# A decoder trunk on one core, its beginning rearranged: memory rows turned unscaled, first weight unit in pieces, small constants later, bias products moved

## The reference

```python
def rmsnorm(x, g):
    y = xf * lax.rsqrt(jnp.mean(xf * xf, axis=-1, keepdims=True) + EPS)
    return (y * g.astype(jnp.float32)).astype(x.dtype)

def rel_bias(table, dist_tok, heads):          # table (32, 12)
    b = table[t5_bucket(dist_tok)][..., heads]
    return jnp.moveaxis(b, -1, 0).astype(jnp.float32)

mem_n = rmsnorm(mem, mem_norm)                 # 256 memory tokens of 1024
for i in range(2):
    hn = rmsnorm(h, norm_mix[i])               # 256 tokens of 1024
    kv = jnp.einsum('bmd,de->bme', mem_n, w_mem_kv[i])     # 1024 x 512
    p  = jnp.einsum('bsd,de->bse', hn, w_in[i])            # layer 0: 1024 x 1408
    # attention with rel_bias, w_out, then the feed-forward part
```

## Time and profile before

| | us |
|---|---|
| median of three runs | 1511.24 |
| profiled execution, time | 1513.64 |
| profiled execution, span of the trace | 1511.8 |
| PE busy | 1475.3 (98%) |
| DVE busy | 1157.4 (77%) |
| ACT busy | 965.2 (64%) |

### The profile page before, as it was taken

The page is one execution under the profiler, slowest core; times in us unless marked ns, Lnnn a source line. Parts: engine busy times, 40 slices in busy tenths (PEclk is TensorE's granted clock), DMA queues, the critical chain, the costliest instruction groups (busy, mean ns, idle before and its releaser), DMA issues.

```text
span 1511.8 us, 19808 instructions
## 1 busy us (share of the span) xinstructions
PE 1475.3 (98%) x7012; PEld 1219.1 (81%) x7012; DVE 1157.4 (77%) x952; ACT 965.2 (64%) x854; POOL 11.0 (1%) x21
## 2 busy tenths in 40 slices
PE   7999999999999999999999999999999999999997
PEld 6888888887778888788888878888878888887885
DVE  4575544454547788988888888888889888888886
ACT  4554444344544677777777777777777777776775
POOL 0100000000000000000000000000000000000000
PEclk9999999999999999999999999999999999999999
DMA  9633555555540499999989999999999998999993
GB/s 350 234 114 126 195 195 179 188 187 171 190 140 17 165 342 365 354 357 373 357 321 363 372 336 364 376 330 355 365 365 338 377 365 314 367 372 334 372 362 125
DMA packets 184096, 433.70 MB, mean 287 GB/s; under 512 B 6963, under 2 KB 8011, under 8 KB 184060
## 3 DMA queue, kind: packets, MB, share of 16 engines
q1 hardware_dynamic: 182048, 426.80, 78.9%
q0 software_dynamic: 1776, 5.84, 1.2%
q10 hardware_dynamic: 236, 0.57, 0.1%
HBM read 432.10 MB, written 1.09 MB: 287 GB/s over the span
## 4 chain that ended last, share of the span: by engine, by line
PE 90%; DVE 5%; ACT 3%; issue 1%; DMA 1%; DVEq 0%; SPq 0%; ACTq 0%
PE ps L1173 27%; PE ps L1175 27%; PE ps L1174 27%; DVE wlo L703 2%; PE ps L1341 2%; ACT whi L428 2%; PE ps L1294 1%; PE ps L1490 1%; PE ps L1267 1%; DMA raw<-in_swa_w_mem_kv 1%; PE ps L1180 1%; PE ps L1280 1%; PE ps L1514 0%; PE ps L1240 0%; PE ps L1519 0%
## 5 line engine op out<-in xcount | busy, mean ns | idle before, releaser
L703 DVE TENSOR_TENSOR wlo<-raw,whi 128x2048 fp32r<-128x2048 f32 x404 | 918.5, 2290 | 241.2 <-ACT whi L428 241.1
L428 ACT ACTIVATE whi<-raw 128x2048 fp32r<-128x2048 f32 x404 | 772.2, 1914 | 251.4 <-PE ps L1175 249.9
L1173 PE MATMUL ps<-whi,xhi 128*128 128x512 f32 x1328 | 519.2, 391 | 6.2 <-DVE wlo L703 5.2
L1175 PE MATMUL ps<-whi,xlo 128*128 128x512 f32 x1328 | 516.0, 389 | 0.0
L1174 PE MATMUL ps<-wlo,xhi 128*128 128x512 f32 x1328 | 515.9, 388 | 0.0
L1173 PEld LDWEIGHTS ps<-whi,xhi 128*128 128x128 f32 x1328 | 249.3, 188 | 62.5 <-DVE wlo L703 10.3
L1175 PEld LDWEIGHTS ps<-whi,xlo 128*128 128x128 f32 x1328 | 249.3, 188 | 51.7
L1174 PEld LDWEIGHTS ps<-wlo,xhi 128*128 128x128 f32 x1328 | 249.4, 188 | 50.2
L1173 PE MATMUL ps<-whi,thi 128*128 128x512 f32 x560 | 224.3, 400 | 7.9 <-DVE tlo L883 7.9
L1175 PE MATMUL ps<-whi,tlo 128*128 128x512 f32 x560 | 218.9, 391 | 0.0
L1174 PE MATMUL ps<-wlo,thi 128*128 128x512 f32 x560 | 218.3, 390 | 0.0
(11 more groups left out here) (175 smaller groups left out, 636.6 us busy)
## 6 DMA issues: line engine op xcount, KB each, us to landing
raw<-in_moe_up SPq DMA_DIRECT2D x112, 1024.0 KB, 6.9
raw<-in_moe_gate SPq DMA_DIRECT2D x112, 1024.0 KB, 6.8
raw<-in_moe_down SPq DMA_DIRECT2D x112, 1024.0 KB, 6.7
raw<-in_ffn_up SPq DMA_DIRECT2D x14, 1024.0 KB, 5.1
raw<-in_ffn_gate SPq DMA_DIRECT2D x14, 1024.0 KB, 5.1
raw<-in_ffn_down SPq DMA_DIRECT2D x14, 1024.0 KB, 4.9
raw<-in_dil_w_in SPq DMA_DIRECT2D x10, 1024.0 KB, 5.1
raw<-in_swa_w_in SPq DMA_DIRECT2D x4, 1024.0 KB, 15.8
```

What stands on the lines that cost most here:

```text
L428: act.activation(whi[:, c % CUT, 0:span(c)], raw[:, c % RAW, 0:span(c)], ACT.Copy).then_inc(hi_ready, 1)
L703: dve.tensor_tensor(wlo[:, c % CUT, 0:n], raw[:, c % RAW, 0:n], whi[:, c % CUT, 0:n].bitcast(F32), ALU.subtract).then_inc(lo_ready, 1)
L1173: pe.matmul(dst, ahi, bhi, start=start, stop=False)
L1175: return pe.matmul(dst, alo, bhi, start=False, stop=stop)
```

## The change

It does the following:

- PE's first products no longer wait for a constant: they multiply a piece of `hn` that DVE has just set to zero, 7 of them.
- The memory rows are transposed as they come from DRAM. The gain is applied after the transposition, when `xhi` and `xlo` are written: there each row block has one gain number per partition. `xhi` and `xlo` are therefore written in 16 instructions of 128 x 128 each (`mem_hi`, `mem_lo`) and not in 4 of 128 x 512. The gain vector comes as 8 rows of 128 numbers and is turned by one small PE transpose; its copy spread over 128 partitions (512 KB) is no longer loaded.
- Unit 0 is loaded in two halves and cut in four quarters, so that its products can start on the first quarter. Chunk 0 runs unit by unit over both tiles and not tile by tile.
- Only the identity and the reversed identity (256 of the 720 columns of `mats`) are loaded first, from ACT. The other constants, the zero-one matrix and the table are issued by POOL, once unit 1 has landed. `eps` is set by DVE.
- The four bias products become two, one for each layer, with their sums over 33 and 99 rows. They stand between chunk 1 and chunk 2, in banks 4 and 5, and chunk 2 waits until ACT has copied them out (`rows_sb`). The copies stand on ACT ahead of `chunk_out(1)`.
- Units 1 and 2 are both cut by `cut_upto(3)`, ahead of the four `norm_root` calls on ACT and ahead of `gained` on DVE.

The core of the diff (the rest are table shapes, semaphores and index changes that follow from it):

```diff
-            load_chunks(0, 1)
+            mk0 = chunk_w["mk0"]
+            sp.dma_start(raw[:, 0, 0:1024].rearrange("p (k f) -> p k f", k=2), mk0[:, 0:2, 0:512]).then_inc(first_in, 16)
+            sp.dma_start(raw[:, 0, 1024:2048].rearrange("p (k f) -> p k f", k=2), mk0[:, 2:4, 0:512])\
+                .then_inc(raw_full[0], 16)
+            load(1, 0, mk0[:, 4:8, 0:512])
             sp.dma_start(h[:, :, :], x[0].rearrange("(t p) d -> p t d", p=P)).then_inc(x_in, 16)
...
-            load_gain(0)
+            pool.wait_ge(raw_full[1], 16)
+            pool.dma_start(onehot[0][:, :], bias_onehot[0:33, 0, 0:RLEN]).then_inc(onehot_in, 16)
+            pool.dma_start(onehot[1][:, :], bias_onehot[:, 1, 0:RLEN]).then_inc(onehot_in, 16)
+            pool.wait_ge(table_one, 2)
+            pool.dma_start(table[0][0:32, :], rel_bias_table).then_inc(table_in, 16)
+            for g in range(3):
+                pool.dma_start(table[1][32 * g:32 * g + 32, 4 * g:4 * g + 4], rel_bias_table[:, 4 * g:4 * g + 4])\
+                    .then_inc(table_in, 16)
+            pool.dma_start(table[1][96:99, :], bias_onehot[96:99, 1, RLEN:]).then_inc(table_in, 16)
+            pool.dma_start(mats[:, 2 * P:], index_mats[:, 2 * P:]).then_inc(const_in, 16)
             pool.dma_start(sm[:, 496:508], bass.AP(swa_sinks.tensor, swa_sinks.offset, [[0, P], [1, NH]]))\
                 .then_inc(sink_in, 16)
-            pool.wait_ge(rows_sb, 4)
-            pool.dma_start(bias_rows[0], rows[0:NH, 0, :]).then_inc(rows_out, 16)
-            for g in range(3):
-                pool.dma_start(bias_rows[1][4 * g:4 * g + 4, :], rows[0:4, 1 + g, :]).then_inc(rows_out, 16)
-            pool.wait_ge(rows_out, 64)
+            pool.wait_ge(rows_sb, 2)
+            for layer in range(2):
+                pool.dma_start(bias_rows[layer], rows[:, layer, :]).then_inc(rows_out, 16)
...
-            act.dma_start(mats[:, :], index_mats).then_inc(const_in, 16)
+            act.dma_start(mats[:, 0:2 * P], index_mats[:, 0:2 * P]).then_inc(ident_in, 16)
+            act.dma_start(gain_rows[:, :], gains[0].rearrange("(k p) -> k p", k=KT)).then_inc(mem_gain_in, 16)
...
+            def mem_hi(half):
+
+                for t in range(TILES):
+                    b = 2 * t + half
+                    act.wait_ge(tr_done, TR0[T_MEM] + b + 1)
+                    for j in range(4):
+                        kt = 4 * half + j
+                        last = act.activation(xhi[:, kt, t * P:(t + 1) * P], ps[:, b, j * P:(j + 1) * P], ACT.Copy,
+                                              scale=mem_gain[:, kt:kt + 1])
+                    last.then_inc(xhi_ready, 1)
...
-            act.wait_ge(const_in, 16)
+            act.wait_ge(ident_in, 16)
             preload(ACT.Sqrt)
-            act.dma_start(onehot[:, :, :], bias_onehot).then_inc(onehot_in, 16)
-            act.dma_start(table[0:32, :], rel_bias_table).then_inc(table_in, 16)
-            for t in range(TILES):
-                xT_hi(T_MEM, t)
-                cut_upto(t + 1)
+            act.wait_ge(mem_gain_turned, 1)
+            act.activation(mem_gain, ps[:, 4, 0:KT], ACT.Copy).then_inc(mem_gain_ready, 1)
+            act.wait_ge(mem_gain_ready, 1)
+            mem_hi(0)
+            for j in range(4):
+                if j < 2:
+                    act.wait_ge(first_in, 16)
+                else:
+                    act.wait_ge(raw_full[0], 16)
+                act.activation(whi[:, 0, j * 512:(j + 1) * 512], raw[:, 0, j * 512:(j + 1) * 512], ACT.Copy)\
+                    .then_inc(first_hi if j < 3 else hi_ready, 1)
+            nxt[0] = 1
+            mem_hi(1)
+            cut_upto(3)
+            act.wait_ge(eps_set, 1)
             for t in range(TILES):
                 act.wait_ge(mem_in[t], 16)
                 norm_root(0, t, memx)
...
             act.wait_ge(chunk_done, 2)
             xT_hi(T_MIX0, 0)
+            for layer in range(2):
+                act.wait_ge(rows_mm, layer + 1)
+                act.activation(rows[:, layer, :], ps[0:NH, 4 + layer, 0:RLEN], ACT.Copy, scale=8.0).then_inc(rows_sb, 1)
             chunk_out(1, memkv[:, 1, 0, :])
             xT_hi(T_MIX0, 1)
             chunk_out(C_SI, proj[:, 0, 0:CHUNKS[C_SI][1]])
-            act.wait_ge(rows_mm, 1)
-            for g in range(4):
-                n = NH if g == 0 else 4
-                act.activation(rows[0:n, g, :], ps[0:n, g, 0:RLEN], ACT.Copy, scale=8.0).then_inc(rows_sb, 1)
             preload(ACT.Exp)
             for c in range(C_SI + 1, C_SO):
                 chunk_out(c, proj[:, 0, CHUNKS[c][3]:CHUNKS[c][3] + CHUNKS[c][1]])
-            act.wait_ge(rows_out, 64)
+            act.wait_ge(rows_out, 32)
             attention(0)
             for t in range(TILES):
...
+            def mem_lo(half):
+
+                dve.wait_ge(mem_gain_ready, 1)
+                for t in range(TILES):
+                    b = 2 * t + half
+                    dve.wait_ge(xhi_ready, TILES * half + t + 1)
+                    for j in range(4):
+                        kt = 4 * half + j
+                        cols = slice(t * P, (t + 1) * P)
+                        last = dve.scalar_tensor_tensor(xlo[:, kt, cols], ps[:, b, j * P:(j + 1) * P],
+                                                        mem_gain[:, kt:kt + 1], xhi[:, kt, cols].bitcast(F32),
+                                                        ALU.mult, ALU.subtract)
+                    last.then_inc(xlo_ready, 1)
...
-            dve.memset(table[32:33, :], 1.0).then_inc(table_one, 1)
-            for t in range(TILES):
-                gained(0, t, memx, mem_in[t], 16)
-            for t in range(TILES):
-                xT_lo(T_MEM, t)
-                cut_upto(t + 1)
+            dve.memset(hn[:, 0, 0:SEQ], 0.0).then_inc(warm_set, 1)
+            dve.memset(eps, EPS).then_inc(eps_set, 1)
+            dve.memset(table[0][32:33, :], 1.0).then_inc(table_one, 1)
+            dve.memset(table[1][:, :], 0.0).then_inc(table_one, 1)
+            mem_lo(0)
+            for j in range(4):
+                if j < 3:
+                    dve.wait_ge(first_hi, j + 1)
+                else:
+                    dve.wait_ge(hi_ready, 1)
+                cols = slice(j * 512, (j + 1) * 512)
+                dve.tensor_tensor(wlo[:, 0, cols], raw[:, 0, cols], whi[:, 0, cols].bitcast(F32), ALU.subtract)\
+                    .then_inc(first_lo if j < 3 else lo_ready, 1)
+            nxt[0] = 1
+            mem_lo(1)
+            cut_upto(3)
             for t in range(TILES):
                 gained(1, t, h, x_in, 16)
...
-                if op is None and not by_tile:
+                if by_unit or op is None and not by_tile:
                     order = [(i, t) for i in range(n_units) for t in range(TILES)]
                 else:
                     order = [(i, t) for t in range(TILES) for i in range(n_units)]
                 for step, (i, t) in enumerate(order):
                     u = FIRST[c] + i
-                    pe.wait_ge(lo_ready, u + 1)
-                    if op is not None:
+                    if u > 0:
+                        pe.wait_ge(lo_ready, u + 1)
+                    if by_unit:
+                        pe.wait_ge(xlo_ready, TR0[op] + step + 1)
+                    elif op is not None:
                         pe.wait_ge(xlo_ready, TR0[op] + t * n_units + i + 1)
                     dst = ps[:, chunk_bank(c, t), 0:width]
                     for j in range(4):
                         kt = 4 * i + j
                         cols = slice(j * width, (j + 1) * width)
+                        if u == 0 and j < 3:
+                            pe.wait_ge(first_lo, j + 1)
+                        elif u == 0:
+                            pe.wait_ge(lo_ready, 1)
...
-            pe.wait_ge(const_in, 16)
-            keep_warm(7, 4)
-            norm_transposed(0, T_MEM, 0)
-            keep_warm(7, 2)
-            norm_transposed(0, T_MEM, 1)
-            keep_warm(7, 4)
-            chunk(0, T_MEM)
+            pe.wait_ge(warm_set, 1)
+            for _ in range(7):
+                pe.matmul(ps[:, 7, 0:SEQ], hn[:, 0, 0:P], hn[:, 0, 0:SEQ], start=True, stop=True)
+            pe.wait_ge(ident_in, 16)
+            pe.wait_ge(mem_gain_in, 16)
+            pe.transpose(ps[:, 4, 0:KT], gain_rows[:, :], ident[0:KT, 0:KT]).then_inc(mem_gain_turned, 1)
+            for t in range(TILES):
+                pe.wait_ge(mem_in[t], 16)
+                transpose_x(T_MEM, t)
+            keep_warm(7, 5)
+            pe.wait_ge(mem_gain_ready, 1)
+            chunk(0, T_MEM, None, False, 0, True)
...
             chunk(1, T_MEM, x_transposed)
+            pe.wait_ge(onehot_in, 32)
+            pe.wait_ge(table_in, 80)
+            pe.wait_ge(table_one, 2)
+            pe.wait_ge(ev_act, ACT_EV[0])
+            pe.wait_ge(ev_dve, DVE_EV[0])
+            for layer in range(2):
```

(49 more changed lines are left out.)

16 lines of the change are left out of this document (9 added, 7 removed).

## The result

The changed kernel takes 1516.39 us, the median of nine runs (1514.66 to 1517.46); the kernel before, beside it, 1511.27 (1511.03 to 1512.94). The ratio is 1.0029, with a 95% interval of 1.0020 to 1.0038: slower, by 5.1 us between the medians and some 4.4 by the ratio. The profiled executions differ by less: 1515.89 and 1513.64, so 2.25 us.

The account below looks back on a forecast made before the run. PE bounds the kernel, so only its late starts and waits count. Chunk 3 1.5 us later at full clock plus 1.7 for one clock fall make 3.2: 1516.8 profiled, 2.4 lower as median, 1514.4 us; range 1511.0 to 1517.1.

Parts of the forecast that it names:

- Head start: PE's first product: about 7 us earlier, at 11 to 12 us; the 16 copies cost at most 6.4 us, hidden.
- Unit 2 takes it away: Unit 2 lands at 21.2 us, ACT waiting; savings 1.3 us, then 1.05 if the slow 10 to 14 us stretch goes.
- Wait before unit 3: PE in chunk 1: a new wait of 2.9 us, from 29.9 until unit 3 is ready at 32.8.
- Wait before chunk 2: PE waits 4.8 us after the bias products, since ACT copies them before cutting unit 4; chunk 2 starts at 47.2.
- Full clock: Start of chunk 3 without clock falls: 58.3 against 56.79, +1.5 us; generally the landing of unit 2 minus 19.7 us.
- The clock: PE's clock halves around the two new waits: cost 0 to 3.4 us, one fall in full taken, 1.7 us.
- rival 2: Clock stays full or falls only within PE's waits: +1.5 us, 1512.7 us; chance 0.27.
- From the profile to the median: Whole kernel: 3.2 us added to the profiled 1513.64 gives 1516.8; the median lies 2.4 lower, 1514.4 us.
- 4 (early landing): Not slower: unit 2 lands early, 1509.7 us if at 18.2; over 0.2% faster only before 16.7; chance 0.13.
- 5 (no head start): First product no earlier than 15 us, from a late gain transpose or late copies; at most 1 us more; chance 0.05.
- Rival 3: Both new waits of PE bring a clock fall: +4.9 us, 1516.1 us; chance 0.17.
- rival 1: One fall of PE's clock in full after the new waits: 1514.4 us; chance 0.38.

Follow-up runs that it names:

- Run 7: Changed kernel with the small constants issued when unit 3 has landed, not unit 1: 1514.61 us, ratio 1.0018 to the kernel before.
- run 2: Changed kernel with only the cut of unit 2 moved back behind the four roots (ACT) and gained x rows (DVE): 1513.50 us, ratio 1.0015.
- run 1: Changed kernel with the two bias products back behind chunk 2, their copies behind its chunk_out on ACT: 1509.56 us, ratio 0.9983.
- run 9: Changed kernel with one line added: ACT cuts unit 4 ahead of the two bias copies: 1511.24 us, ratio 0.9996.
- run 3: Changed kernel with bias products back behind chunk 2 and the roots ahead of the cut of unit 2: 1506.63 us, ratio 0.9969.
- run 10: Changed kernel, nothing altered, profiled a third time: 1517.14 us, one execution.
- run 4: Changed kernel with nine more idle products on PE behind the bias products, in the wait before chunk 2: 1513.51 us, ratio 1.0013.
- run 5: Kernel before the change, nothing altered, profiled once more: 1511.06 us, one execution.
- run 6: Changed kernel, nothing altered, profiled a second time: 1515.20 us, one execution.

## Why the prediction was right, and where its sizes were off

- **Head start, first product at 11 to 12 us.** Right, 11.92. The 16 copies took 4.4 us together (two rows of 2.17 and 2.22), 0.27 each and not 0.40; they were hidden, as forecast: ACT was through with unit 1 at 15.9 and waited for unit 2.
- **Unit 2 takes it away.** Right: the cut of unit 2 was released by its transfer. It came at 19.9 and not 21.2: from 10 to 14 us 413 GB/s moved, not the 293 of the earlier trace rows, so the second step of that term held in full, and the first 8 us gave a little more (349 and not 342 GB/s). By these two rates alone it would be near 20.4; the other half microsecond stays open. Run 7 showed the price, one us for each us, and that the small constants delay unit 2 by 1.1 us.
- **Wait before unit 3.** Forecast 2.9 us, measured 2.50; run 2 shows that it is the order of the cut and the roots.
- **Wait before chunk 2.** Forecast 4.8, measured 4.89; runs 1 and 9 show that it is the copies ahead of the cuts on ACT. The prediction wanted to see both waits released by `wlo`; the view names `memkv` for this one, wrongly, as said above.
- **The two bias products.** Forecast 1.34 us from start to start, measured 1.49 (49.18 to 50.67 in run 3; 1.56 is the listed duration). 99 rows cost no more than 33: 490 and 486 ns per pass.
- **Full clock.** The rule "landing of unit 2 minus 19.7" gives +0.2 with 19.9. Measured: 2.38 at the start of attention less the 2.0 of the fall, +0.4.
- **The clock.** One fall in full, 1.7 us, was forecast, and at most 3.4 us for two. The one behind the second wait was in all three profiles; it was 6.8 us long, twice the one near 478 us, with a quarter to two fifths of it inside the wait, and cost 2.0 to 2.4. The one behind the first wait was in one of three and cost 1.6. Both together, in run 10, cost 4.0. The Trainium skill's rule of long gaps (TensorE: Matmul & The Clock Gate, HAM oscillation) held here for the wait of 4.9 us, and run 4 shows it: with the gap filled the clock stays. The falls behind 2.5 us, and behind 1.55 us near 478 us, come after waits shorter than the gaps which that section describes; that they exist is shown by these profiles alone.
- **A misreading in rival 2.** The prediction says that in the first 20 us the clock stayed full through waits of about 1.5 us. That holds for the wait before 18.41 only. The views print 1.00 up to there, but PE's rows show half the clock until about 14 us:

```profile
5.31 3.78 PE L1180 MATMUL ps<-mats 128*128 128x256 f32 x8 [5.31 <-DMA mats<-in_index_mats]
10.67 1.97 PE L1192 MATMUL ps<-mats,hn 128*128 128x128 f32 x8 [1.58 <-DVE hn L723]
12.43 1.84 PE L1180 MATMUL ps<-mats 128*128 128x256 f32 x4
14.11 1.04 PE L1192 MATMUL ps<-mats,hn 128*128 128x128 f32 x8
14.98 1.89 PE L1180 MATMUL ps<-mats 128*128 128x256 f32 x8
```

Eight transposes take 1.97 us and then 1.04; four passes take 1.84 and then eight take 1.89. The wait of 1.58 us fell into a time when the clock was low already, so it says nothing for rival 2.

- **From the profile to the median.** This is the term that was mis-sized. I took the difference from the one profiled execution of before and carried it to the median. That execution had started 1.56 us late, by the landing of unit 0, and in it the clock fell near 478 us. The change makes all from chunk 1 on hang on unit 2 (cut between 19.75 and 20.14 in seven profiles of five kernels) and no longer on unit 0 (12.6 or 14.1), so against a kernel before that starts on time, as in run 5, the 1.6 us count in full: +0.4 + 2.0 + 1.6 = 4.0, measured between run 6 and run 5 4.1, and up to 1.9 more where the clock falls twice. The medians differ by 5.1, so in the median execution of the changed kernel probably a second fall came on top, behind the first wait or near 480 us. The mean granted clocks of whole executions hint at it: the six slowest of the nine runs, the median among them, are listed with 0.995, the other three with 0.996, and run 10 has 0.995, run 6 0.996. It is no more than a hint, since run 7 has a second fall near 480 us and 0.996. The forecast said 3.2. Of this 1.3 was too much for unit 2; missing were 1.6 for the start, about 0.3 in the size of the fall and about 1 for a second one. The right sign rests on the mechanism; that the number came as near as it did is in part luck, errors of opposite sign.
- **Rivals.** Rival 2 (clock stays), 4 (early landing) and 5 (no head start) are out for the median. Rival 3, both waits with a fall, occurred in run 10, and the measured median, 1516.39, is nearer to its 1516.1 than to the 1514.4 of rival 1. That does not decide between them, since both numbers lack the 1.6 us of the start: run 6, with the one fall of rival 1, took 1515.20.

What stays open: when exactly the clock falls behind a wait of 2.5 us (it did in one of three profiles of the changed kernel, and in three of the seven of all kernels with that wait), which falls the median execution had, and what moves the landing of unit 0 in the kernel before.

## What to carry to other kernels

Where one engine prepares what the bounding engine eats, its program order is the schedule: before moving a product, look what its result's reader has queued behind it, and cut the next unit first. A head start is worth only what the next transfer in the queue leaves of it; look for the last landing that the chain needs before spending effort on the first. And before a difference is carried from a profile to a median, see in a second profile whether the first was a typical execution: here 1.5 us in the start and 1.1 in the middle were not.

## What the runs showed of the hardware

- With a wait of PE of 4.9 us came 6.8 us at half clock, beginning inside the wait, in all five profiles that have it unfilled (three of the changed kernel, runs 2 and 7); nine idle products in the same wait kept the full clock (run 4). Behind a wait of 2.4 to 2.5 us came 3.4 us at half clock in three profiles (runs 1, 4 and 10) and none in four. Waits of 1.53 and 1.54 us before unit 2 (runs 2 and 3) and one of 2.23 us before unit 0 (run 5) were not followed by a fall. The wait near 478 us is of 1.54 or 1.55 us in all 13 profiles, behind a stretch with many short products; the clock fell there in five of them, and in some executions of the same kernel only. The first profile of the changed kernel and run 6 show it:

```profile
480.51 2.01 PE L1261 MATMUL ps<-mats,hn 128*128 128x128 f32 x8 [1.55 <-DVE hn L878]
```

```profile
480.73 1.16 PE L1261 MATMUL ps<-mats,hn 128*128 128x128 f32 x8 [1.54 <-DVE hn L878]
```

- A granted clock of 1.00 at the beginning of a span is no evidence. In the first profile of the kernel before, PE's products ran at half speed until about 14 us (rows above) where the views print 1.00; in run 5 the first eight passes took 3.69 us and four at 11.03 took 1.03, so the full clock came earlier.
- Some 0.45 MB of small transfers (rows of 16 bytes to 1.9 KB), issued beside the weights, delayed a 1 MB unit by 1.1 us (run 7), about what their bytes alone take at 397 GB/s.
- A copy of 128 x 128 from PSUM with a gain per partition took 0.27 us on ACT, in a row of eight, and the product and difference of that size 0.27 us on DVE. 512 columns in one instruction cost 0.5 us; in four pieces, 1.1.
